# Grouping the rows of an expert sum four at a time instead of two on TensorE

## The chip, the cores and the metric

The kernel runs on one core of one Trainium2 chip. The metric is the device time of one execution in microseconds (us). Its engines run side by side, each through an instruction list of its own in a fixed order, and meet only at semaphores: TensorE (PE, its weight loads PEld), VectorE (DVE), ScalarE (ACT), GpSimd (POOL) and SyncE (SP), which issues DMAs.

## The reference

One decoder layer over 512 prompt tokens and 32 new tokens. Convolution and sparse attention are merged and normed to `h`; behind that stands the channel mixer, whose last lines the change is about. Each token picks 128 of 16384 experts:

```python
def peer_ffn(x2, peer_w_query, peer_keys1, peer_keys2, peer_u, peer_v):
    qh = jnp.einsum('nd,dhk->nhk', x2, peer_w_query)
    ...
    g = jax.nn.softmax(ts, axis=-1)
    u = peer_u[eidx]
    v = peer_v[eidx]
    a = jax.nn.gelu(jnp.einsum('nd,nhed->nhe', x2, u).astype(jnp.float32), approximate=False)
    return jnp.einsum('nhe,nhed->nd', (g * a).astype(v.dtype), v)
```

`u` and `v` are 128 rows of 1024 numbers for each token.

## The kernel before

The tokens are five tiles: four of 128 prompt tokens (0 to 3) and one of 32 new ones (`S_T`). For each tile a front computes projections, convolution and attention, a tail forms `h` (the products with `w_conv_out` and `w_out`, L1404, then the query product with `w_query`, L1524, and the key products, L1539), and a routing on VectorE (from L2009 on) picks the experts of the 8 heads, one head after the other.

**The gathers.** Each tile then needs 128 `peer_u` fetches (one for each expert slot, for all 128 tokens at once) and 128 `peer_v` fetches (one for each token, its 128 expert rows). Each fetch is 128 x 1024 numbers, 0.524 MB, written by one indirect DMA that GpSimd issues at L906 into a place of a ring of 11 (`PLACES`) in SBUF. Below, a row is one such fetch, row i of tile v is ("v", v, i). A `u` row is used up by one VectorE instruction (L2232), a `v` row by TensorE in `expert_pair` (L1820): the token's 128 weights, in one column of a 128 x 32 block that is zero elsewhere, times the 128 x 512 halves of the row, added into PSUM partitions `32*j` to `32*j + 31` with `j = i % 4`. So four rows in sequence go to four different column quarters of the array. Every such product of float32 runs as two passes, so a pair of rows is 8 passes.

**Who may go on.** GpSimd waits before each fetch until the earlier row in the same place has been used (`dotted` or `summed`). TensorE waits for the rows' landing (`row_in`) and, at the first row of four, for `diag_ready`: ScalarE has then copied the weights of that group of four into its block (`column`, L1293), for which it waits in turn until the group two before has been summed.

**The order.** `fetches` writes the queue by hand: the 128 `u` rows of tile 0, then 80 `v` rows of tile 0 alone (`EARLY_V[0]`), then `u` rows of tile 1 mixed with the other `v` rows of tile 0, then 32 `v` rows of tile 1 alone, the mix of tiles 2 and 1, 32 `v` rows of tile 2 alone, the mix of tiles 3 and 2, 32 `v` rows of tile 3, and the rest. While the 80, 32 and 32 rows stand alone, the front and tail of the next tile run: no `u` row can be fetched before the routing of its tile. Every engine merges its strands (fronts, tails, `mixer`) by estimated times at build, so that TensorE's list has a pair of rows between every few matmuls of the tail. GpSimd's list follows the queue.

In the profile's names `rings` is the ring, `acc` the PSUM sum, `z_stages` holds the weight blocks, `late` the expert numbers, `uah` the transposed `h`.

## Time and profile before

| | |
|---|---|
| median of 3 runs | 2096.13 us (2087.34 to 2105.51) |
| the profiled execution | 2089.12 us |
| its span, first to last instruction | 2087.3 us |
| TensorE busy | 1449.6 us |
| VectorE busy | 1282.2 us |
| GpSimd busy | 1205.3 us |
| moved by DMA | 682.74 MB, 327 GB/s over the span |
| granted TensorE clock, mean | 0.84 of 2.4 GHz |

No engine is busy all the time; which one holds up the others changes from stage to stage, so the table has to be read with stretches of the trace. The execution that was profiled lies 7 us under the median.

### The profile page before, as it was taken

To read this page: it belongs to the slowest core of one execution; us is meant where nothing else is said; L and a number is where in the kernel's file an instruction comes from. 1 tells how busy PE (TensorE), PEld (TensorE's weight loads), DVE (VectorE), ACT (ScalarE), POOL (GpSimd) and SP (SyncE) were. 2 spreads that over 40 slices of the span, in tenths; PEclk is the share of its full clock that TensorE was granted. 3 is DMA by queue.
4 is the path that set the end of the run, shared out by engine and by line. 5 is a ranking of instruction groups with operands and counts; after the bars stand their busy time and mean duration, and the time that the engine had idled before them with its cause. 6 is when DMAs were issued, how large, how long until landed. Compare 5 with 4: busy or idle time off the path is not lost.

```text
span 2087.3 us, 19495 instructions
## 1 busy us (share of the span) xinstructions
PE 1449.6 (69%) x6117; PEld 578.3 (28%) x6117; DVE 1282.2 (61%) x3076; ACT 381.6 (18%) x1031; POOL 1205.3 (58%) x1107
## 2 busy tenths in 40 slices
PE   7899999778975657676658777855354356766435
PEld 3554444333320214342112332411111012221101
DVE  4429964881178499848949767577399974112341
ACT  1510011372000352110027221100010002100000
POOL 1003454485566658756766777677576665336664
PEclk9999999988997885688789878997575568889869
DMA  8728999799989978989999899999999979979997
GB/s 305 315 87 304 327 357 367 261 307 324 324 312 341 378 243 296 363 295 329 352 404 336 312 344 372 329 364 373 307 362 349 370 261 392 382 249 358 378 364 293
DMA packets 207458, 682.74 MB, mean 327 GB/s; under 512 B 26901, under 2 KB 54933, under 8 KB 200787
## 3 DMA queue, kind: packets, MB, share of 16 engines
q0 software_dynamic: 157376, 581.67, 76.4%
q1 hardware_dynamic: 42971, 90.66, 12.2%
q10 hardware_dynamic: 7008, 9.17, 1.2%
q8 instruction: 49, 0.80, 0.2%
q14 instruction: 54, 0.44, 0.1%
HBM read 668.88 MB, written 12.94 MB: 327 GB/s over the span
## 4 chain that ended last, share of the span: by engine, by line
PE 33%; DVE 19%; POOL 15%; issue 13%; DMA 8%; SPq 7%; ACT 2%; another core or an unknown queue 2%; POOLq 0%; ACTq 0%; DVEq 0%
POOL rings L906 15%; PE acc L1820 8%; DVE rings L2232 7%; PE acc L1380 7%; DMA rings<-peer_v,late 6%; PE wide L1380 3%; PE bank L1524 3%; DVE small L1884 3%; SPq L707 3%; PE wide L1404 2%; PE acc L1347 2%; SPq L715 2%; DVE uah L1887 1%; DVE soft_score L1887 1%
## 5 line engine op out<-in xcount | busy, mean ns | idle before, releaser
L906 POOL DMA_INDIRECT rings<-peer_u,late x544 | 611.8, 1125 | 428.6 <-DVE late L2232 166.7
L1820 PE MATMUL acc<-rings,z_stages 128*32 128x512 f32 x2048 | 554.5, 704 | 397.6 <-issue 211.4
L906 POOL DMA_INDIRECT rings<-peer_v,late x544 | 585.0, 1075 | 341.2 <-PE acc L1820 154.2
L2232 DVE CUSTOM_DVE_ANT_0 rings<-rings,uah 128x1024 f32<-128x1024 f32 x288 | 346.7, 1224 | 151.6 <-DMA rings<-peer_u,late 136.5
L2232 DVE CUSTOM_DVE_ANT_0 rings<-rings,late 128x1024 f32<-128x1024 f32 x256 | 308.6, 1223 | 99.3 <-DMA rings<-peer_u,late 94.6
L1820 PEld LDWEIGHTS acc<-rings,z_stages 128*32 128x32 f32 x2048 | 120.1, 120 | 771.0 <-issue 763.6
L1380 PE MATMUL acc<-rings 128*128 128x512 f32 (+1 forms) x352 | 147.3, 569 | 0.0
L1293 ACT COPY z_stages<-late 128x4 f32<-128x4 f32 x136 | 26.2, 198 | 523.0 <-PE acc L1820 329.9
L1553 PE MATMUL wide<-zt,ident_s 128*128 128x512 f32 x122 | 73.2, 700 | 20.9 <-issue 11.7
L1380 PEld LDWEIGHTS acc<-rings 128*128 128x128 f32 x352 | 62.5, 190 | 69.6 <-issue 68.9
L1667 PE MATMUL wide<-keep,soft_score 128*128 128x64 f32 x320 | 57.8, 335 | 33.3 <-ACT soft_score L1112 31.2
L1043 ACT ACTIVATE zt<-uah,conv_p 128x128 f32<-128x128 f32 x244 | 76.7, 390 | 18.8 <-PE wide L1553 14.4
L1347 PE MATMUL acc<-rings 128*128 128x512 f32 (+2 forms) x176 | 69.0, 540 | 14.4 <-DMA small<-quarter 12.2
L1380 PE MATMUL wide<-rings,uah 128*128 128x512 f32 (+1 forms) x176 | 74.4, 564 | 0.0
L1667 PEld LDWEIGHTS wide<-keep,soft_score 128*128 128x128 f32 x320 | 51.1, 241 | 70.6 <-ACT soft_score L1112 56.9
L1524 PE MATMUL bank<-uah,w_query_s 128*128 128x128 f32 x512 | 63.6, 281 | 1.5 <-ACT uah L1070 1.4
L1524 PEld LDWEIGHTS bank<-uah,w_query_s 128*128 128x128 f32 x512 | 59.8, 194 | 14.8 <-issue 12.4
L1404 PE MATMUL wide<-w_out_s,uah 128*128 128x512 f32 x128 | 62.5, 637 | 1.4 <-ACT uah L1063 0.7
L1097 ACT ACTIVATE soft_score<-soft_score,small 128x128 f32<-128x128 f32 (+3 forms) x64 | 35.6, 557 | 128.0 <-DVE small L2097 119.0
L1553 PE MATMUL wide<-z_stages,ident_s 128*128 128x512 f32 x64 | 38.3, 683 | 29.6 <-ACT z_stages L1043 28.5
L2009 DVE MAX8 uah<-zt 128x8 f32<-128x128 f32 x68 | 19.3, 284 | 63.7 <-PE bank L1524 49.3
L1636 PE MATMUL bank<-keep,queries 64*128 64x128 f32 (+3 forms) x128 | 54.2, 563 | 0.0
(298 smaller groups left out, 1594.4 us busy)
## 6 DMA issues: line engine op xcount, KB each, us to landing
rings<-w_in SPq DMA_DIRECT2D x36, 1024.0 KB, 7.5
rings<-peer_u,late POOLq DMA_INDIRECT x544
rings<-peer_v,late POOLq DMA_INDIRECT x544
z_rows<-z_stages ACTq DMA_DIRECT2D x30, 256.0 KB
soft_score<-ln SPq DMA_DIRECT2D x6, 1024.0 KB
zt<-z_rows SPq DMA_DIRECT2D x2, 2596.0 KB
w_out_s<-w_out POOLq DMA_DIRECT2D x1, 4096.0 KB, 17.0
w_query_s<-w_query POOLq DMA_DIRECT2D x1, 4096.0 KB, 14.0
```

The source lines that it names most:

```text
L707: return sp.value_load(page_s[0:1, at:at + 1], min_val=0, max_val=N_POOL - 1)
L906: nc.gpsimd.indirect_dma_start(ring[:, place, :], None, table, offs).then_inc(row_in[place], 16)
L1043: last = nc.scalar.activation(scaled_of(t, k)[:, c, :], uT3[:, c, k:k + P], ACT.Copy, scale=cp[:, c, k:k + 1])
L1347: last = nc.tensor.matmul(acc[:, i % 2 * BLK + lo:i % 2 * BLK + hi], xT_0[:, k, :], w[:, c, :], start=(k == 0), stop=(k == KC - 1))
L1380: last = nc.tensor.matmul(z_bank[j][:, 0:width], x[j][:, m, :], w[:, c, :], **flags)
L1404: last = nc.tensor.matmul(dst[0:n, half * BLK:(half + 1) * BLK], lhs[:, c, 0:n], rhs[:, c, half * BLK:(half + 1) * BLK], start=(c == 0), s ...
L1524: last = nc.tensor.matmul(s_bank[hd // 4][:, hd % 4 * P:(hd % 4 + 1) * P], wqu[:, c, hd * PEER_DQ:(hd + 1) * PEER_DQ], aT3[:, c, :], start ...
L1553: nc.tensor.matmul(wide[:, BLK:], ident[:, :], scaled_of(t, k).rearrange("p c n -> p (c n)"), start=(k == 0), stop=(k == CONV_W - 1), skip ...
L1667: last = nc.tensor.matmul(wide[:, o * HEAD_DIM:(o + 1) * HEAD_DIM], pt2[:, g % 2, at * P:(at + 1) * P], v3[:, j, kv * HEAD_DIM:(kv + 1) * ...
L1820: last = nc.tensor.matmul(acc_v[QUAD * j:QUAD * (j + 1), half * BLK:(half + 1) * BLK], lone[:, quad % LONE, j, QUAD - 1 - m:2 * QUAD - 1 - m],
L1884: chain.link(V.max(top, values))
L2232: V.tensor_tensor_reduce(out=ring[:, place, :], in0=ring[:, place, :], in1=h, scale=1.0, scalar=0.0, op0=ALU.mult, op1=ALU.add, accum_out= ...
```

## The change

The 80, 32 and 32 `v` rows of tiles 0, 1 and 2 that stand alone in the queue are multiplied in groups of four: TensorE reaches the group at the place where the second pair stood, waits there for all four rows, and issues the first halves of the four and then the second halves. All other rows, the 32 of tile 3 too, stay in pairs. The semaphore `summed` goes up once for each row as before.

```diff
+    def rows_at_once(v, i):
+
+        return N_QUADS if v < LAST and i < EARLY_V[v] else N_QUADS // 2
+
...
-        def expert_pair(v, i):
+        def expert_rows(v, i, count):
...
-            for k in (i, i + 1):
+            for k in range(i, i + count):
                 place, landed, _ = HOMES["v", v, k]
                 pe.wait_ge(row_in[place], landed)
...
             for half in range(2):
-                for k in (i, i + 1):
+                for k in range(i, i + count):
...
-                    if number % 2:
-                        expert_pair(tile, number - 1)
+                    count = rows_at_once(tile, number)
+                    if number % count == count - 1:
+                        expert_rows(tile, number - count + 1, count)
```

The new lines shift the numbers behind them by 4: L1404 becomes L1408, L1524 L1528, L1820 L1824.

TensorE's list at the start of tile 1's tail, where the transposes of the convolution's norm (L1472, L1479) and the product with `w_conv_out` stand. A row here is a run of matmuls of one line; `x4` at L1820 is a pair of rows (two rows, two halves). Before:

```order
L1667 MATMUL wide<-keep,soft_score 128x64 x4
L1472 MATMUL bank<-ident_s,queries 128x128 x4
L1820 MATMUL acc<-rings,z_stages 32x512 x4
L1479 MATMUL bank<-ident_s,soft_score 128x128 x4
L1820 MATMUL acc<-rings,z_stages 32x512 x4
L1404 MATMUL wide<-w_conv_out_s,conv_acc 128x512 x2
L1820 MATMUL acc<-rings,z_stages 32x512 x4
```

And now:

```order
L1671 MATMUL wide<-keep,soft_score 128x64 x4
L1476 MATMUL bank<-ident_s,queries 128x128 x4
L1483 MATMUL bank<-ident_s,soft_score 128x128 x4
L1824 MATMUL acc<-rings,z_stages 32x512 x8
L1408 MATMUL wide<-w_conv_out_s,conv_acc 128x512 x4
L1824 MATMUL acc<-rings,z_stages 32x512 x8
```

The first pair of each four has moved down to the second: the transposes now stand next to each other, and four matmuls of the product stand between groups where two stood between pairs.

TensorE's list at the end of the same tail, in the query product of tile 1. Before:

```order
L1524 MATMUL bank<-uah,w_query_s 128x128 x12
L1820 MATMUL acc<-rings,z_stages 32x512 x4
L1524 MATMUL bank<-uah,w_query_s 128x128 x8
L1820 MATMUL acc<-rings,z_stages 32x512 x4
L1524 MATMUL bank<-uah,w_query_s 128x128 x4
L1539 MATMUL bank<-peer_keys_s,queries 128x128 x8
L1524 MATMUL bank<-uah,w_query_s 128x128 x8
L1820 MATMUL acc<-rings,z_stages 32x512 x4
L1524 MATMUL bank<-uah,w_query_s 128x128 x8
L1820 MATMUL acc<-rings,z_stages 32x512 x8
L1539 MATMUL bank<-peer_keys_s,queries 128x128 x8
L1820 MATMUL acc<-rings,z_stages 32x512 x112
```

And now:

```order
L1824 MATMUL acc<-rings,z_stages 32x512 x8
L1528 MATMUL bank<-uah,w_query_s 128x128 x12
L1543 MATMUL bank<-peer_keys_s,queries 128x128 x8
L1528 MATMUL bank<-uah,w_query_s 128x128 x8
L1824 MATMUL acc<-rings,z_stages 32x512 x8
L1528 MATMUL bank<-uah,w_query_s 128x128 x8
L1824 MATMUL acc<-rings,z_stages 32x512 x8
L1543 MATMUL bank<-peer_keys_s,queries 128x128 x8
L1824 MATMUL acc<-rings,z_stages 32x512 x112
```

Ahead of the last piece of the query product stand 15 groups of four now, and stood 30 pairs before: the same 60 rows.

TensorE's list in the query product of tile 2, with the rows of tile 1. Before:

```order
L1820 MATMUL acc<-rings,z_stages 32x512 x4
L1524 MATMUL bank<-uah,w_query_s 128x128 x16
L1820 MATMUL acc<-rings,z_stages 32x512 x4
L1524 MATMUL bank<-uah,w_query_s 128x128 x12
L1820 MATMUL acc<-rings,z_stages 32x512 x4
L1524 MATMUL bank<-uah,w_query_s 128x128 x12
L1820 MATMUL acc<-rings,z_stages 32x512 x4
L1524 MATMUL bank<-uah,w_query_s 128x128 x8
L1539 MATMUL bank<-peer_keys_s,queries 128x128 x8
L1524 MATMUL bank<-uah,w_query_s 128x128 x4
L1820 MATMUL acc<-rings,z_stages 32x512 x4
L1524 MATMUL bank<-uah,w_query_s 128x128 x12
```

And now:

```order
L1528 MATMUL bank<-uah,w_query_s 128x128 x16
L1824 MATMUL acc<-rings,z_stages 32x512 x8
L1528 MATMUL bank<-uah,w_query_s 128x128 x24
L1824 MATMUL acc<-rings,z_stages 32x512 x8
L1528 MATMUL bank<-uah,w_query_s 128x128 x8
L1543 MATMUL bank<-peer_keys_s,queries 128x128 x8
L1528 MATMUL bank<-uah,w_query_s 128x128 x16
```

Five pairs stood ahead of the end of the query product; two groups of four do now, and the fifth pair has become part of the group behind it. In tile 3's query product three pairs stood there and one group does.

## Rows read from the trace of the kernel before

**Rows 1.** The page: engines' busy time, and the chain that ended last.

```profile
PE 1449.6 (69%) x6117; PEld 578.3 (28%) x6117; DVE 1282.2 (61%) x3076; ACT 381.6 (18%) x1031; POOL 1205.3 (58%) x1107
...
PE 33%; DVE 19%; POOL 15%; issue 13%; DMA 8%; SPq 7%; ACT 2%; another core or an unknown queue 2%; POOLq 0%; ACTq 0%; DVEq 0%
```

**Rows 2.** The page's groups: busy and mean ns, then idle before and its releaser.

```profile
L1820 PE MATMUL acc<-rings,z_stages 128*32 128x512 f32 x2048 | 554.5, 704 | 397.6 <-issue 211.4
L906 POOL DMA_INDIRECT rings<-peer_v,late x544 | 585.0, 1075 | 341.2 <-PE acc L1820 154.2
```

**Rows 3.** Windows: us, busy of PE, PEld, DVE, ACT, POOL, PEclk, DMA share, GB/s.

```profile
480.00:600.00 120.00, 110.92 (x558) 44.55 (x556) 27.58 (x83) 17.90 (x40) 65.78 (x70) 1.00 0.88 314
...
900.00:960.00 60.00, 46.82 (x275) 26.19 (x277) 26.67 (x82) 10.42 (x23) 30.72 (x30) 0.84 0.80 276
```

**Rows 4.** Timeline of TensorE in tile 1's tail: start, us, instruction, passes, idle before.

```profile
501.63 1.98 PE L1404 MATMUL wide<-w_conv_out_s,conv_acc 128*128 128x512 f32 x4
503.55 1.91 PE L1820 MATMUL acc<-rings,z_stages 128*32 128x512 f32 x8
...
547.99 1.94 PE L1820 MATMUL acc<-rings,z_stages 128*32 128x512 f32 x16
...
580.79 1.91 PE L1820 MATMUL acc<-rings,z_stages 128*32 128x512 f32 x8
582.63 2.05 PE L1524 MATMUL bank<-uah,w_query_s 128*128 128x128 f32 x16
```

**Rows 5.** Windows of line L1820 alone, up to the query product's last piece.

```profile
480.00:582.70 102.70, 52.62 (x240) 10.92 (x240) 1.00 0.89 320
```

**Rows 6.** Timeline of VectorE: the routing of tile 1 begins.

```profile
584.72 0.30 DVE L2009 MAX8 uah<-zt 128x8 f32<-128x128 f32 x1 [31.48 <-PE bank L1524]
```

**Rows 7.** Timeline of GpSimd: rows 10 and 11 of tile 0.

```profile
476.68 0.94 POOL L906 DMA_INDIRECT rings<-peer_v,late  x1 [0.30 <-issue]
482.81 0.93 POOL L906 DMA_INDIRECT rings<-peer_v,late  x1 [5.19 <-PE acc L1820]
```

**Rows 8.** Timeline of GpSimd: row 79 of tile 0, first `u` row of tile 1.

```profile
598.58 0.94 POOL L906 DMA_INDIRECT rings<-peer_v,late  x1 [1.65 <-PE acc L1820]
599.82 0.94 POOL L906 DMA_INDIRECT rings<-peer_u,late  x1 [0.30 <-issue]
```

**Rows 9.** Windows of all engines, columns as in rows 3, where the mix runs.

```profile
600.00:620.00 20.00, 11.20 (x42) 2.50 (x40) 17.80 (x62) 0.59 (x3) 14.14 (x15) 0.91 0.99 368
...
680.00:720.00 40.00, 25.66 (x104) 8.11 (x104) 16.40 (x32) 14.11 (x37) 25.49 (x27) 0.85 1.00 393
```

**Rows 10.** The chain that ended last, in order of time: waits for a landing.

```profile
988.27 6.14 DMA rings<-peer_v,late
...
1056.09 12.75 DMA rings<-peer_v,late
```

**Rows 11.** Timeline of TensorE in tile 2's query product.

```profile
914.96 2.91 PE L1820 MATMUL acc<-rings,z_stages 128*32 128x512 f32 x8
...
921.57 1.91 PE L1820 MATMUL acc<-rings,z_stages 128*32 128x512 f32 x8
...
937.55 1.91 PE L1820 MATMUL acc<-rings,z_stages 128*32 128x512 f32 x8
939.40 2.94 PE L1524 MATMUL bank<-uah,w_query_s 128*128 128x128 f32 x24
```

**Rows 12.** Timeline of GpSimd: the first `u` row of tile 2.

```profile
960.14 0.93 POOL L906 DMA_INDIRECT rings<-peer_u,late  x1 [0.30 <-issue]
```

**Rows 13.** Timeline of TensorE in tile 3's query product.

```profile
1322.65 2.17 PE L1820 MATMUL acc<-rings,z_stages 128*32 128x512 f32 x8
...
1333.08 1.91 PE L1820 MATMUL acc<-rings,z_stages 128*32 128x512 f32 x8
1334.92 2.05 PE L1524 MATMUL bank<-uah,w_query_s 128*128 128x128 f32 x16
```

**Rows 14.** Timeline of GpSimd: the first `u` row of tile 3.

```profile
1361.85 0.94 POOL L906 DMA_INDIRECT rings<-peer_u,late  x1 [0.30 <-issue]
```

## The prediction

> **What bounds the kernel now.** I read the page first. No engine is busy throughout, and the chain that ended last runs over TensorE for 33% of the span, VectorE for 19%, GpSimd for 15% [rows 1]: the bound changes with the stage, so the change is worth what it is worth in the stages it touches. The groups name its line: the products of the `v` rows are the dearest group of TensorE, and GpSimd's `v` fetches stood idle for 154.2 us because `acc` L1820 had not given back a place [rows 2].
>
> Then the stage in which the 80 rows stand alone. From 480 to 600 us TensorE is busy for 110.92 of 120 us, VectorE for 27.58, GpSimd for 65.78, and DMA moves 314 GB/s [rows 3]. The timeline shows a rhythm: a piece of the tail's product, 1.98 us, a pair of rows, 1.91 us, and again with no gap [rows 4]. Meanwhile VectorE waits 31.48 us for the query product before the routing of tile 1 can begin at 584.72 [rows 6], and the rows fill the ring and wait: after row 10 GpSimd stood idle for 5.19 us until a pair gave back its places [rows 7]. So TensorE is the bound from 481 to 585 us, with the tail of tile 1 behind it, on which the routing, and through it all later `u` rows, depend. What shortens TensorE's list here moves everything behind it. From 600 us on the picture is another: the DMA engines are 0.99 to 1.00 busy at 368 to 393 GB/s [rows 9].
>
> **The cost of a group of four.** A pair has 8 passes and takes 1.91 us. In a few places the list has pairs next to each other with their rows landed, and there 16 passes take 1.94 us [rows 4]: the four column quarters already work at once when TensorE has four rows in hand. A group of four is exactly that, so I take 1.94 us for it, against 3.8 us for two pairs that are apart. The products per row, their passes and the 512-column width don't change.
>
> The Trainium skill, TensorE: Matmul & The Clock Gate, under Part 3: Packing small matmuls, reports less than full scaling for such packing: 2.38 times with three column tiles of 32 and 3.07 times with four row tiles. An estimate by that page: a group of four would take some 2.4 us rather than 1.94, and the gain worked out below would be about 7 us smaller. The x16 row here says the packing is nearly free in this kernel, and the sum goes by the row.
>
> **Tile 1's tail, step by step.** Up to the last piece of the query product, which starts at 582.63 [rows 4], 240 passes of L1820, 30 pairs, are busy for 52.62 us [rows 5]; that includes those that already overlap. Fifteen groups at 1.94 us are 29.1 us: **23.5 us less**. Not all of it arrives. In two places (the convolution's norm and the norm of `h`) TensorE waits for VectorE and ScalarE, and pairs had filled that time; the first pair of a four has now moved behind the wait. I charge one group, 2 us: 21.5 us.
>
> Next comes the supply of rows. With TensorE faster, rows 11 to 59, which waited for their places from 482.81 us on [rows 7], must land some 20 us sooner. They are 49 x 0.524 = 25.7 MB, and the tail's own loads (`x_rows`, `ln1`) 1.6 MB. At the 368 GB/s of the near-saturated window [rows 9] that takes 74 us and ends at 557 us, and TensorE now wants row 59 at about 559: just in time. In the middle it is not: TensorE wants row 47 after some four fifths of the gain, at about 538 us, and rows 11 to 47 with the loads, 21 MB, need 57 us from 482.8, so 540. Places that come back four at a time add some. A tail delayed there stays delayed. I charge 3.5 us and take **18 us** for the start of the routing. The bounds: 21.5 if the supply keeps up, and below, if the queue gives only the 314 GB/s of the stage now, nearly nothing, since rows 11 to 59 would land at 570 us and the last piece follow at about 576: 8 us.
>
> GpSimd must arrive as well, since the first `u` row of tile 1 stands behind row 79. It was issued at 599.82, 117 us after row 11 [rows 7, 8]. Rows 11 to 79 and the loads are 37.8 MB, 103 us at 368 GB/s, so row 79 lands at 586, is issued some 6 us before that [rows 10], and the `u` row follows at 581: 19 us sooner. Both paths agree, so 18 us. VectorE has 31.48 us of idle time there [rows 6] and only starts sooner. GpSimd issues no more and no fewer fetches.
>
> **Tile 2.** Here 32 rows stand alone, and DMA has room: 0.80 busy, 276 GB/s [rows 3]. The end of the query product has five pairs ahead of it, the first 2.91 us long, four of 1.91, and two groups of four after the change: 10.6 less 3.9 is 6.7 us [rows 11]. For GpSimd: row 11 goes out when the first group ends, at about 921; from there a group needs the place that the group two before it gives back, plus an issue, a landing of 6.1 us [rows 10] and 1.94 us, so two groups take 8.5 us. That is quicker than GpSimd issues eight rows, 10 us at 0.94 and 0.30 us each [rows 7]. With the row that has to wait for its place each time, 21 issues from 921 on take some 33 us: the first `u` row of tile 2 goes out at 954 in place of 960.14 [rows 12]. I take **6 us**.
>
> **Tile 3.** Three pairs (2.17 and twice 1.91 us) stood ahead of the last piece of the query product, and one group does: 6.0 less 1.94 is 4.1 us [rows 13]. GpSimd gets row 11 out about 2 us later than now, since the first places come back with the second pair's time, and makes it up: by the same steps its `u` row goes out 4 to 5 us before 1361.85 [rows 14]. I take **4 us**.
>
> **What costs nothing.** ScalarE's `column` waits for the group two before; that stands at the same point of TensorE's list as before, because a group ends where its second pair ended. The later use of a group's first two rows delays those places by a pair's slot, which is in the sums above. The rows that aren't grouped keep their instructions. What lies behind the three stretches is bound by queues whose beginnings all move (routing, rows, front of the next tile), so I see no place that holds a clock of its own, and let the gains add up.
>
> **The sum.** 18 + 6 + 4 = 28 us off the profiled execution's 2089.1: 2061. The median lies 7 us higher, so **2068 us**.
>
> **Rivals.**
>
> *The ring is too small for groups of four* (slower). Of 11 places a waiting group holds four, and the last row of a group can be issued only when the group two before has been summed. The rate is then one landing plus an issue and a product for eight rows. At 6.1 us that is harmless, but landings of 12.75 us occur under load [rows 10]: (12.75 + 0.3 + 1.94) / 8 is 1.87 us a row, against 116 us for 68 rows now, 1.70 a row [rows 7, 8]. Pairs in the same ring depend on a landing for ten rows and don't suffer. The point from which it decides is a landing of about 11.4 us. If they all were 12.75: 69 rows x 0.17 + 64 x 0.1 is +18 us, 2114 us. For it speaks that TensorE frees the DMA to run into its own saturation, where landings lengthen; against it, that a landing in the mix, at such rates, still takes 6.14 us [rows 10].
>
> *The DMA takes the gain of the first stage.* The stage's 314 GB/s at a DMA share of 0.88 [rows 3] leaves a factor of 1.14 by share: 357 GB/s rather than 368, and bursts of four lose some. Then stage one gives about 8 us and the others 3 each: 14 us, 2082.
>
> *The gain is given back later.* The mix is bound by DMA and VectorE; if one of them has slack that only the late start of the stage hides, the 28 us shrink to about 15: 2081. I count it with the one before.
>
> *The change doesn't do what it says.* If TensorE overlapped the pairs wherever it matters already, nothing would move: 2096. Against it stands 52.62 us for 30 pairs [rows 5], 1.75 us each, where full overlap would be 0.97.
>
> **How the numbers follow.** Forecast (gain 22 to 34 us): 0.55. DMA or later stages take part (gain 8 to 21 us): 0.27. Nothing moves: 0.11. The ring makes it slower: 0.07. The range is to hold 8 in 10: at the low end the unhindered sum, 21.5 + 6.7 + 5 = 33 us, and a few us because runs of one kernel differ by up to 9 us from their median: 2055. At the high end the case of a partial gain down to 8 us: 2089. A change within 1%, 21 us, can hardly be told from none in this kernel. Faster by over 1%: 0.56; within 1%: 0.40, with the partial gain, no effect and most of the slower case; slower by over 1%: 0.04.
>
> **What would show it.** In the new profile L1824 should show 16 passes in 1.94 us in the first stretch, four matmuls of the product between them; the first MAX8 of tile 1 at about 567 us in place of 584.72, and the first `u` row of tile 1 at about 581; GpSimd's idle time for `acc` well under 154 us; a DMA rate near 360 GB/s from 480 to 580. The `u` rows of tiles 2 and 3 should come 24 and 28 us sooner than now. I am wrong if a group takes clearly over 2 us, if TensorE waits for landings in that stretch for more than about 5 us in all, or if the lead at 600 us has melted by 960.

## The result, and where the time went

The changed kernel takes 2089.18 us (median of 19 runs, 2067.47 to 2097.94), the kernel before, on the same chip, 2098.74 (19 runs, 2087.34 to 2109.32). The ratio is 0.9948, 95% interval 0.9928 to 0.9969: by that ratio it is 10.9 us faster, 6.5 to 15.1 by the interval, where 28 were forecast (the two medians alone are 9.6 us apart). The profiled execution took 2084.76 us (span 2083.0) against 2089.12 for that of before.

The page of the changed kernel, parts 1, 4 and 5 (columns as in [rows 1, 2]; the line numbers have moved by four):

```profile
PE 1420.0 (68%) x6117; PEld 573.4 (28%) x6117; DVE 1281.0 (61%) x3076; ACT 381.4 (18%) x1031; POOL 1219.3 (59%) x1107
...
PE 33%; DVE 21%; POOL 13%; issue 12%; DMA 10%; SPq 7%; ACT 2%; another core or an unknown queue 2%; ACTq 0%; POOLq 0%; DVEq 0%
...
L1824 PE MATMUL acc<-rings,z_stages 128*32 128x512 f32 x2048 | 526.5, 741 | 410.7 <-DMA rings<-peer_v,late 220.2
L910 POOL DMA_INDIRECT rings<-peer_v,late x544 | 586.2, 1077 | 321.2 <-issue 138.7
```

GpSimd's idle time before `v` fetches is no longer put down to `acc` in the first place (119.4 us where it was 154.2, and 27.4 us more that the view can't attribute), and the landings of rows have become what TensorE's products wait for most.

In the stretch of the 80 rows TensorE's timeline reads:

```profile
502.79 1.92 PE L1824 MATMUL acc<-rings,z_stages 128*32 128x512 f32 x16
504.65 3.70 PE L1408 MATMUL wide<-w_conv_out_s,conv_acc 128*128 128x512 f32 x8
508.28 1.92 PE L1824 MATMUL acc<-rings,z_stages 128*32 128x512 f32 x16
...
528.21 1.92 PE L1824 MATMUL acc<-rings,z_stages 128*32 128x512 f32 x16 [1.64 <-DMA rings<-peer_v,late]
530.07 3.70 PE L1408 MATMUL wide<-w_out_s,uah 128*128 128x512 f32 x8
534.26 1.93 PE L1824 MATMUL acc<-rings,z_stages 128*32 128x512 f32 x16 [0.50 <-DMA rings<-peer_v,late]
```

A group of four takes 1.92 us, with two pieces of the tail's product between groups instead of one. New are the waits for landings: 0.50 to 1.64 us, four of them up to 546 us (two are shown), 4.8 us in all. The windows of the same kernel, with the columns of [rows 3]:

```profile
500.00:520.00 20.00, 19.53 (x97) 7.05 (x96) 2.76 (x4) 1.76 (x6) 12.70 (x14) 0.99 0.97 351
...
480.00:600.00 120.00, 95.12 (x570) 43.72 (x572) 33.14 (x100) 17.88 (x41) 72.58 (x76) 0.87 0.94 344
```

From 480 to 600 us TensorE is busy for 95.12 us where it was 110.92 [rows 3], and the DMA engines have gone from 0.88 and 314 GB/s to 0.94 and 344. VectorE's first MAX8 of tile 1, by the timeline:

```profile
575.43 0.29 DVE L2014 MAX8 uah<-zt 128x8 f32<-128x128 f32 x1 [32.14 <-PE bank L1528]
```

It is 9.3 us sooner than in [rows 6]. The first `u` rows of tiles 1, 2 and 3 go out at 591.8, 951.4 and 1353.7 us: 8.1, 8.7 and 8.1 us sooner than in [rows 8, 12, 14]. So the first stretch gives some 8 us and the other two add nothing to it.

Positions in the whole execution carry what happened before them: the issue of row 0 of the 80 came at 463.9 us here and at 460.0 in the kernel before, 3.9 us apart before anything of the change runs. I therefore compare stretches from their own row 0. From the issue of row 0 of `v(0)` to the first MAX8 of tile 1 ("first stretch" from here on) it is 124.7 us before and 111.5 after: 13.2 us, not 9.3. It is this figure against the 18 us forecast, and the two short stretches against their 10, that the experiments take apart.

### The profile page after: what moved, and what is told of

The parts are those of the page before. It is cut to its first block, busy times and chain, and to the rows that moved or that the text cites. A ratio compares the mean times of both kernels' runs of the same rounds, so it can differ in the third digit from the quotient of the medians.

```text
span 2083.0 us, 19494 instructions
## 1 busy us (share of the span) xinstructions
PE 1420.0 (68%) x6117; PEld 573.4 (28%) x6117; DVE 1281.0 (61%) x3076; ACT 381.4 (18%) x1031; POOL 1219.3 (59%) x1107
## 4 chain that ended last, share of the span: by engine, by line
PE 33%; DVE 21%; POOL 13%; issue 12%; DMA 10%; SPq 7%; ACT 2%; another core or an unknown queue 2%; ACTq 0%; POOLq 0%; DVEq 0%
POOL rings L910 13%; DVE rings L2237 8%; PE acc L1824 7%; DMA rings<-peer_v,late 7%; PE acc L1384 7%; PE bank L1528 3%; PE wide L1384 3%; DVE small L1889 3%; SPq L711 3%; PE wide L1408 3%; PE acc L1351 2%; DVE uah L1892 2%; SPq L719 2%; DVE soft_score L1892 1%
## 5 line engine op out<-in xcount | busy, mean ns | idle before, releaser
L910 POOL DMA_INDIRECT rings<-peer_u,late x544 | 624.7, 1148 | 436.0 <-DVE late L2237 168.6
L1824 PE MATMUL acc<-rings,z_stages 128*32 128x512 f32 x2048 | 526.5, 741 | 410.7 <-DMA rings<-peer_v,late 220.2
L1824 PEld LDWEIGHTS acc<-rings,z_stages 128*32 128x32 f32 x2048 | 111.1, 124 | 770.7 <-issue 765.7
L1528 PE MATMUL bank<-uah,w_query_s 128*128 128x128 f32 x512 | 65.3, 290 | 5.7 <-issue 5.0
L1528 PEld LDWEIGHTS bank<-uah,w_query_s 128*128 128x128 f32 x512 | 63.1, 204 | 13.7 <-issue 12.3
L1408 PE MATMUL wide<-w_out_s,uah 128*128 128x512 f32 x128 | 60.7, 627 | 1.5 <-ACT uah L1067 0.7
```

What stands on the lines that cost most here:

```text
L910: nc.gpsimd.indirect_dma_start(ring[:, place, :], None, table, offs).then_inc(row_in[place], 16)
L1408: last = nc.tensor.matmul(dst[0:n, half * BLK:(half + 1) * BLK], lhs[:, c, 0:n], rhs[:, c, half * BLK:(half + 1) * BLK], start=(c == 0), s ...
L1528: last = nc.tensor.matmul(s_bank[hd // 4][:, hd % 4 * P:(hd % 4 + 1) * P], wqu[:, c, hd * PEER_DQ:(hd + 1) * PEER_DQ], aT3[:, c, :], start ...
L1824: last = nc.tensor.matmul(acc_v[QUAD * j:QUAD * (j + 1), half * BLK:(half + 1) * BLK], lone[:, quad % LONE, j, QUAD - 1 - m:2 * QUAD - 1 - m],
```

## The experiments

They ran on four chips, which differ (whether the result's own is one of them isn't recorded): the kernel before took 2091.6 us on the first, 2050.6 on the second, 2047.9 on the third, and 2103.1 and 2099.8 (two sessions) on the fourth. Ratios are to the kernel before on the same chip, in brackets the 95% interval.

### Which of the three stretches gives the gain

`only80` groups in the first stretch alone, `only32s` in the two short ones alone (`only80_b` and `only32s_b` are the same kernels on another chip):

```
-        return N_QUADS if v < LAST and i < EARLY_V[v] else N_QUADS // 2
+        return N_QUADS if v == 0 and i < EARLY_V[v] else N_QUADS // 2        # only80
+        return N_QUADS if 0 < v < LAST and i < EARLY_V[v] else N_QUADS // 2  # only32s
```

> Only the 80 rows of tile 0 go in groups of four; the 32 and 32 rows of tiles 1 and 2 stay in pairs. In the trace of the changed kernel tile 0's stretch brought 8 of the 10 us. If the gains of the three stretches add up and stay, this kernel is 6 to 8 us faster than before (ratio 0.996 to 0.997). If a lead won in one stretch is used up by the next one's waits (the rival: later stages take it back), it is under 3 us.

> Only the 32 rows of tile 1 and the 32 of tile 2 go in groups of four; the 80 of tile 0 stay in pairs. If the stretches add up, this is 3 to 6 us faster than before, and with the other kernel it sums to the 10 us of the full change. If holding four places of eleven costs as much as the shorter TensorE list brings, it is 0 to 2 us.

> Groups of four for the 80 rows of tile 0 alone, again, since chips differ (the kernel before took 2091.6 us on one and 2050.6 on another) and times scatter less on the faster one. If the 80 rows carry all of the gain, the ratio is that of the full change on such a chip, 0.991 on the fast one or 0.992 to 0.995 on the slow one; if the stretches add up it is 3 to 6 us short of it.

> Groups of four for the 32 rows of tiles 1 and 2 alone, again. Additive stretches as I had forecast them: 0.995. Theory now (the fetches, not TensorE's list, set the pace there): 0.998 to 1.000.

Measured: only80 2079.78 us, 0.9922 (0.9891 to 0.9954), and only80_b 2034.67 us, 0.9931 (0.9908 to 0.9955). only32s 2090.32 us, 0.9990 (0.9964 to 1.0016), and only32s_b 2048.29 us, 0.9994 (0.9972 to 1.0016). only80 gained 12 to 16 us where 6 to 8 were expected: within the intervals the whole effect is the first stretch's. The two short ones together give 1.3 us on one chip and nothing on the other, and by the intervals no more than 6 to 8.

`tail_only` takes the groups only as far as tile 1's tail has work for TensorE (64, 12 and 12 rows):

```
-        return N_QUADS if v < LAST and i < EARLY_V[v] else N_QUADS // 2
+        return N_QUADS if v < LAST and i < (64, 12, 12)[v] else N_QUADS // 2
```

> Groups of four only as long as the tail's matmuls stand between the rows: rows 0 to 63 of tile 0 and 0 to 11 of tiles 1 and 2; the rows behind the tail, where TensorE has time and the fetches set the pace, go in pairs. Theory one (the gain was lost in the first stretch to TensorE's half clock and to the supply of rows): the same as the full change within 3 us. Rival (groups hold places where the fetches set the pace): 5 us or more faster than the full change, so 15 us faster than before, with the first u row of tile 2 some 4 us further ahead of where it was.

Measured: 2084.22 us, 0.9934 (0.9900 to 0.9968), no different from only80 within the intervals. Groups behind the tail, where only rows are left on TensorE, add nothing that these runs can tell.

### Does TensorE's clock take it back

In the changed kernel the granted clock fell to half in this stretch (0.75 in the window 480 to 500 and 0.83 in 540 to 560, where the kernel before showed no half clock from 481 to 600): TensorE now has gaps. `gap_pairs` leaves pairs where the gaps are, so that rows fill them; `filler` is the changed kernel with passes over a block of zeros in the gaps, which add zero to `acc`:

```
+        in_gap = v == 0 and (8 <= i < 12 or 40 <= i < 52)
-        return N_QUADS if v < LAST and i < EARLY_V[v] else N_QUADS // 2
+        return N_QUADS if v < LAST and i < EARLY_V[v] and not in_gap else N_QUADS // 2   # gap_pairs
...
+            for _ in range(k):                                                           # filler
+                nc.tensor.matmul(acc[:, 0:BLK], zero, w_out[:, 0:BLK], start=False, stop=False, skip_group_check=True)
```

> As the full change, but rows 8 to 11 and 40 to 51 of tile 0 stay in pairs, so that TensorE has a pair to do while it waits for the convolution's norm and for the norm of h, and its clock need not fall there (in the changed kernel it fell to 0.5 at 490.0, 544.6 and 551.5 us, in the kernel before nowhere from 481 to 600). If the lost part of the first stretch is the half clock, the routing of tile 1 starts 3 to 5 us sooner than in the full change (575.4 us) and the kernel is some 4 us faster than it. If the supply of rows was the limit, TensorE only waits longer for rows afterwards and nothing is won: within 2 us of the full change.

> The full change, with nine matmuls of a zero block (they add 0 to acc) ahead of tile 1's waits for the convolution's norm (five), for h (two) and for h's copies (two), so that TensorE is busy where it idles now. The output is unchanged. Theory one, the half clock costs: the clock stays at 1.0 from 480 to 580, the group behind the norm takes 1.9 us and not 3.64, the product behind it 3.7 and not 4.76, and the routing of tile 1 starts 3 to 5 us sooner, at 571. Rival, the supply of rows is the limit: the clock stays up but TensorE waits as much longer for rows, and the routing starts where it did, within 1.5 us.

> The changed kernel itself once more, on the same chip as the next three. By its own 19 runs it should stand at 0.995 of the kernel before; the first routing of tile 1 in its trace at 572 to 577 us and TensorE's clock at 0.5 for 7 to 17 of the 100 us from 480 on.

Measured: gap_pairs 2084.32 us, 0.9954 (0.9924 to 0.9984). filler 2033.21 us, 0.9921 (0.9896 to 0.9945), beside the changed kernel itself, full_again, at 2033.15 us, 0.9914 (0.9897 to 0.9932). The window of filler:

```profile
480.00:580.00 100.00, 90.55 (x561) 43.02 (x559) 24.82 (x73) 17.68 (x39) 64.50 (x67) 0.98 0.95 368
```

and of full_again:

```profile
480.00:580.00 100.00, 84.58 (x532) 39.00 (x524) 26.28 (x78) 17.67 (x39) 64.88 (x68) 0.92 0.95 362
```

The filler keeps the clock up (0.98 for 0.92), and the first stretch changes from 105.9 to 104.4 us, the time not at all. So on this chip the half clock costs at most some 1.5 us. On a chip where `before` takes 2091.6 us, gap_pairs has 0.96 from 480 to 580 us where the changed kernel's own profile has 0.91, and its first stretch is no shorter (112.4 against 111.5 us). The clock falls where TensorE waits; it isn't why it waits. That theory falls, the 4 us of gap_pairs and the 3 to 5 of filler with it. full_again also gained more (0.9914) than the 0.995 that was expected of it: the chips differ in the gain too, which a later section takes up.

### Does the supply of rows take it back

`half_pairs` and `half_groups` are the kernel before and the changed one with every row of the three stretches fetched in its first half only: 512 of 1024 columns, half the bytes. TensorE multiplies as many columns as before, partly of other values:

```
+            half = f[0] == "v" and f[1] < LAST and f[2] < EARLY_V[f[1]]
+            if half:
+                table = table.rearrange("e (k d) -> (e k) d", k=2)
+            nc.gpsimd.indirect_dma_start(ring[:, place, 0:D_MODEL // (1 + half)], None, table,
+                                         offs).then_inc(row_in[place], 16)
```

> The kernel before, but the 80, 32 and 32 rows that stand alone are fetched as 512 numbers for each token instead of 1024 (from the table seen as 512 wide, so other values), and the second half of the product uses what lies in the ring: half the bytes in the three stretches, the same instructions. TensorE was the bound there, so nothing before 585 us should change: routing of tile 1 at 582 to 585 us, and the kernel within 5 us of before or a few us faster where the rows behind the tail come sooner.

> The changed kernel with the same 144 rows fetched as 512 numbers for each token (half the bytes, other values, the same instructions). If the supply of rows cost the first stretch its gain, TensorE no longer waits for landings, the clock stays up, and the routing of tile 1 starts at 562 to 566 us, some 20 us ahead of the pairs with half rows. If the clock and the waits for VectorE and ScalarE are what costs, it stays at 570 to 575 us.

Measured, on the chip of full_again: half_pairs 2050.34 us, 0.9993 (0.9976 to 1.0010): with pairs the bytes don't matter at all, as the prediction had it. half_groups 2021.96 us, 0.9850 (0.9827 to 0.9873), 28.6 us below this kernel before by the medians, against 17.5 for full_again. Its first routing starts at 565.1 us, where the theory of the supply expected 562 to 566. Its window:

```profile
480.00:580.00 100.00, 86.52 (x558) 40.30 (x556) 27.19 (x81) 18.07 (x41) 66.79 (x69) 0.95 0.66 196
```

The same halving in one place each, by the condition `f[1] == 0` (groups_half80) and `0 < f[1] < LAST` (groups_half32s):

> The full change, with half the bytes for the 80 rows of tile 0 only (rows of 512 numbers, other values). The full change with half the bytes for all 144 rows gained 28.6 us, the full change with whole rows 17.4 on the same chip. If the missing 11 us were lost in the first stretch, this kernel gains 25 us or more; if they were lost in the two short ones, some 18.

> The full change, with half the bytes for the 32 rows of tile 1 and the 32 of tile 2 only. The counterpart: some 18 us if the loss lies in the first stretch, 25 or more if it lies in the short ones, about 22 in each if it is shared.

Measured, on the third chip: groups_half80 2026.66 us, 0.9896 (0.9867 to 0.9924), groups_half32s 2027.83 us, 0.9894 (0.9863 to 0.9926); some 21 and 20 us faster than `before`: neither the 25 for one place nor the 18 for the other, but the case in which the loss is shared. The changed kernel didn't run beside them; only80_b did, with 0.9931, and its interval overlaps with both. So a few us in each place are likely and not shown by the times. Read by stretches it is small: the first stretch takes 104.4 to 105.9 us with whole rows (four traces) and 102.5 and 102.7 with half of them, so the supply holds it up by some 2.4 us.

`extra_pairs` and `extra_groups` turn the test round and add load: behind tile 1's norm loads SyncE issues eight copies of 0.52 MB within the DRAM, for which nothing waits but the end.

```
+            if t == 1:
+                for k in range(8):
+                    sp.dma_start(spare[k], io["peer_u"][P * k:P * (k + 1)]).then_inc(spare_in, 16)
```

> The kernel before, and behind the norm loads of tile 1 SyncE issues eight copies of 0.52 MB within the DRAM, in the stretch of the 80 rows; nothing waits for them but the end. It takes from the DMA engines 4.2 MB read and written, beside 42 MB of rows. Theory of the supply: with pairs TensorE sets the pace and rows land early (the waits for landings in the stretch are small), so the routing of tile 1 starts less than 4 us later than in the kernel before, where it started 124.7 us after v(0,0), and the time stays within 0.3% of before. Theory that the supply doesn't matter to either kernel: the same.

> The changed kernel with the same eight copies in the same place. Theory of the supply: with groups of four the rows set the pace in the stretch, so that all the time that the copies take from the DMA engines shows: 8.4 MB more to move at some 380 GB/s are 20 us of the engines if reads and writes both count and 10 us if only one does, and the routing of tile 1 starts 8 to 16 us later than without them (105 to 112 us after v(0,0)), which takes away most of the gain: ratio 0.995 to 1.001. Theory that TensorE's clock or the issue of the rows on GpSimd set the pace: under 4 us later, and the ratio stays at that of the changed kernel, 0.991 to 0.995.

Measured: extra_pairs 2103.13 us, 1.0012 (0.9990 to 1.0034); extra_groups 2095.62 us, 0.9963 (0.9933 to 0.9993). In the traces the first stretch takes 126.8 us with pairs, 2.1 more than in the kernel before, and 127.7 with groups, 12 more than in the trace of the changed kernel on the same chip (full_third, below) and 12 to 18 more than in all traces of groups on such chips. TensorE in extra_groups:

```profile
508.40 3.64 PE L1830 MATMUL acc<-rings,z_stages 128*32 128x512 f32 x16 [5.30 <-DMA rings<-peer_v,late]
...
517.63 1.92 PE L1830 MATMUL acc<-rings,z_stages 128*32 128x512 f32 x16 [1.46 <-DMA rings<-peer_v,late]
...
522.75 3.20 PE L1830 MATMUL acc<-rings,z_stages 128*32 128x512 f32 x16 [2.17 <-DMA rings<-peer_v,late]
```

Three of its four waits for landings are shown, of 9.3 us in all; with pairs there is one, of 0.7 us. So the pairs have slack in the supply and the groups have next to none: more load lands on their path at once. The traced execution of extra_groups was one of its longer ones, 9.3 us above its median, and the median lost only some 6 us against full_third (0.9935, below) on the same chip, with intervals that overlap; 12 us is therefore an upper figure.

### Why the chips differ

`half_groups_b` is half_groups again, on the fourth chip:

> The changed kernel with every peer_v row of the three lone stretches fetched in its first half only (512 of 1024 columns; TensorE multiplies the same number of columns as before, from other values), as in the run before. Theory of the supply: what is left after the halving doesn't depend on the chip's DMA rate, so the ratio is 0.984 to 0.988 and the first routing starts 101 to 104 us after v(0,0) on any chip, also where the changed kernel gains least. If the chips differ by something else (TensorE's clock, semaphores), this run shows it: 106 us or more.

Measured: 2083.03 us, 0.9912 (0.9878 to 0.9945), and 109.4 us for the first stretch, not 102.7. This is the other answer: with the DMA engines at 0.62 from 480 to 580 us, 7 us are still missing that the supply can't have taken. The timeline shows where they go. First half_groups, at the end of the product with `w_out`: TensorE's last piece and the VectorE step that waits for it.

```profile
531.41 1.98 PE L1412 MATMUL wide<-w_out_s,uah 128*128 128x512 f32 x4
...
533.32 1.92 PE L1828 MATMUL acc<-rings,z_stages 128*32 128x512 f32 x16
...
533.51 0.69 DVE L1957 SCALAR_TENSOR_TENSOR uah<-uah,wide 128x512 f32<-128x512 f32 x1 [9.63 <-PE wide L1412]
...
537.97 1.78 PE L1471 MATMUL bank<-ident_s,uah 128*128 128x128 f32 x8 [2.72 <-DVE uah L1968]
```

and half_groups_b in the same place:

```profile
533.56 1.98 PE L1412 MATMUL wide<-w_out_s,uah 128*128 128x512 f32 x4
...
536.10 1.92 PE L1828 MATMUL acc<-rings,z_stages 128*32 128x512 f32 x16 [0.56 <-issue]
...
540.36 0.69 DVE L1957 SCALAR_TENSOR_TENSOR uah<-uah,wide 128x512 f32<-128x512 f32 x1 [11.61 <-remote]
...
544.82 1.97 PE L1471 MATMUL bank<-ident_s,uah 128*128 128x128 f32 x8 [6.79 <-DVE uah L1968]
```

The piece's record ends at 533.39 and VectorE starts 0.1 us later; on the other chip the record ends at 535.54 and VectorE starts at 540.36, 4.8 us later, the releaser unknown to the view ("remote"). At the end of the first half of the same product ScalarE's `column` and a GpSimd fetch, which wait for groups, and VectorE's step start within 0.11 us of each other, when the pass that VectorE needs has been over for 4.3 us by its record (523.02):

```profile
527.28 0.20 ACT L1301 COPY z_stages<-late 128x4 f32<-128x4 f32 x1 [7.81 <-remote]
527.33 0.69 DVE L1957 SCALAR_TENSOR_TENSOR uah<-uah,wide 128x512 f32<-128x512 f32 x1 [18.76 <-remote]
527.39 0.95 POOL L913 DMA_INDIRECT rings<-peer_v,late  x1 [2.72 <-remote]
```

The ends of matmuls are modelled in these records; here three engines say that TensorE was done later than its records, or that its signals came late. The records can't tell the two apart.

I measured that lag at these two places (start of the VectorE step less the recorded end of the last pass it needs; first and second half of `w_out`) in all traces:

```
pairs, all four chips and the first profile (5 traces)             0.0 and 0.1 in each
groups, chips where before takes some 2050 us (6 traces)           0.0 and 0.1 in each
groups, chips where before takes 2090 to 2103 us:
  changed kernel 2.6, 0.1   only80 0.0, 0.5     tail_only 2.8, 4.0
  gap_pairs      0.0, 1.7   first_pairs 0.0, 2.2   extra_groups 0.2, 1.0
  half_groups_b  4.3, 4.8   zero_groups 0.0, 2.3   full_third 0.0, 2.0
```

At these two places it comes only with groups on these chips. Over whole traces late releases come with these chips, with pairs too, and more of them with groups. "remote" stands where the view finds no recorded end in the 1.5 us before the semaphore changed, and this kernel has no other core to wait for. Nearly all such semaphores here are TensorE's; 1 to 5 in a trace are VectorE's. Counted are waits of over 0.15 us:

```
waits that end with "remote"       whole trace     in the first stretch
chips at ~2050, pairs and groups   0 in all eight  0
other chips, before, extra_pairs   45, 50          1, 2
             only32s               29              1
             groups in the first   51 to 81        1 in extra_groups, 7 to 14 in eight
```

The one in the first stretch of the kernel before is a GpSimd fetch, whose semaphore changed 2.5 us after the recorded end of the pair it waits for:

```profile
564.99 0.94 POOL L906 DMA_INDIRECT rings<-peer_v,late  x1 [2.23 <-remote]
```

So groups aren't needed for the lateness. With pairs it is there and falls seldom into this stretch; with groups it falls there 7 to 14 times, but for extra_groups. The first stretch is longer where it does:

```
first stretch, us                  chips at ~2050              chips at 2090 to 2103
pairs                              122.0, 125.8                124.5, 124.7
groups, whole rows                 104.4, 104.7, 104.9, 105.9  109.4, 111.5, 112.4, 113.4, 114.4, 115.8
groups, half rows                  102.5, 102.7                109.4
```

(gap_pairs and first_pairs, with some pairs left, stand with 112.4 and 113.4; groups_half32s with 104.9.)

Within the right column the length does not follow the lag of the two places: tail_only has a lag of 4.0 us and the shortest stretch, only80 has 0.5 and one of the longest. Of the 7.8 us between the two kinds of chips (112.8 on the mean of six, 105.0 of four) only half, 3.9, has been lost when that VectorE step starts; the other half is lost behind it, in the query product, 35.9 us on the mean up to the MAX8 where the other chips take 32.0. The result's own trace has lost only some 1.3 us at that step (74.3 us after row 0, 73.0 on the mean) and 5.2 behind it, some 3 of these before the query product starts, at the copies of the transposed `h` for which it waits. The transposes (L1467) end by their record at 544.00:

```profile
542.68 1.32 PE L1467 MATMUL bank<-ident_s,uah 128*128 128x128 f32 x8 [1.40 <-DVE uah L1964]
...
546.31 0.58 ACT L1074 COPY uah<-bank 128x512 f32<-128x512 f32 x1 [4.58 <-remote]
549.85 0.58 ACT L1074 COPY uah<-bank 128x512 f32<-128x512 f32 x1 [2.96 <-remote]
```

The second copy starts 5.85 us after that end; in the traces of the other kind of chip it is 0.04 with groups and 0.08 with pairs.

`zero_groups` asks whether it is the load that four quarters at once put on TensorE: in the three stretches both operands of every pass come from a block of zeros (the rows are fetched and waited for, their products left out). `full_third` is the changed kernel beside it.

```
+                                            zero[:, 0:QUAD] if quiet else
                                             lone[:, quad % LONE, j, QUAD - 1 - m:2 * QUAD - 1 - m],
+                                            zero.unsqueeze(1).to_broadcast([P, N_QUADS, P]) if quiet else
                                             ring[:, place, half * BLK:(half + 1) * BLK], start=False,
```

> The changed kernel, in the three lone stretches with both operands of every peer_v pass taken from a block of zeros (same shapes, count, order, waits and releases; the rows are fetched and waited for as before, but their products are left out). Theory of TensorE falling behind its records: in the seven traces of groups of four on chips where this program takes some 2090 us, the VectorE step that waits for the product with w_out starts up to 2.6 to 4.8 us after the recorded end of that product, or the fetches that wait for a group start up to 2.5 us late, and in no trace of pairs, and in none of groups on chips where the program takes some 2050 us, is it over 0.1. If that is the load that four quarters at once put on TensorE, passes over zeros end on time: on such a chip the lateness of L1957 is 0.1 us and the first routing starts 104 to 107 us after v(0,0) instead of 111 to 113. If the lateness comes with the order or count of the passes and not with what they multiply, it stays. On a chip without the lateness both kernels are the same, 104 to 106 us.

> The changed kernel as it is, beside zero_groups on the same chip: 111 to 113 us from v(0,0) to the first routing and a ratio of 0.993 to 0.997 where TensorE falls behind its records, 104 to 106 us and 0.990 to 0.992 where it doesn't.

Measured: zero_groups 2087.02 us, 0.9942 (0.9923 to 0.9961), full_third 2081.72 us, 0.9935 (0.9913 to 0.9958); first stretch 115.8 us in both, lag 2.3 and 2.0. The zeros change nothing: the load of these passes isn't the cause. What makes the releases late on these chips stays open. The records show no cause in the instruction queues' transfers either: the code fetches of this stretch are as many on both kinds of chips and take about 1 us each on either.

### Why the short stretches bring nothing

With groups the first places of the ring come back after row 3 instead of row 1. `first_pairs` leaves the first four rows of each stretch in pairs:

```
-        return N_QUADS if v < LAST and i < EARLY_V[v] else N_QUADS // 2
+        return N_QUADS if v < LAST and N_QUADS <= i < EARLY_V[v] else N_QUADS // 2
```

> The changed kernel, but the first four rows of each of the three lone stretches stay in pairs, all others of them in fours. Theory of the late first release: with groups of four the first places of the ring come back after row 3 and not after row 1, so that GpSimd issues row 11 some 1.5 to 4 us later than before (22.7 us after row 0 before, 26.9 in the changed kernel, in tile 1; 17.0 and 18.4 in tile 2). If that is what keeps the 32-row stretches from giving anything, the u row of tile 2 comes some 2 us sooner after v(1,0) than in the changed kernel (56 to 57 us instead of 58.9), that of tile 3 about 1 us sooner, and the ratio to the kernel before is 0.989 to 0.992 on a chip where the changed kernel has 0.991 to 0.995. Theory of the supply: GpSimd then only waits for the same rows a little later in the stretch, and the time is that of the changed kernel, to 0.2%.

Measured: 2098.83 us, 0.9981 (0.9954 to 1.0009), and 62.0 us from row 0 of `v(1)` to the first `u` row of tile 2, where 56 to 57 were expected. Row 11 did go out sooner, 21.5 us after row 0 where full_third on the same chip has 26.2, and the `u` row didn't follow (61.6 there). The theory of the late first release falls.

The timeline of GpSimd shows where the gain goes, in two traces without late releases. First full_again, with groups, from the last long wait for a place to the first `u` row of tile 2:

```profile
913.99 0.94 POOL L910 DMA_INDIRECT rings<-peer_v,late  x1 [4.58 <-PE acc L1824]
...
930.72 0.94 POOL L910 DMA_INDIRECT rings<-peer_v,late  x1 [1.79 <-PE acc L1824]
931.96 1.24 POOL L910 DMA_INDIRECT rings<-peer_u,late  x1 [0.30 <-issue]
```

and half_pairs, with pairs and half rows:

```profile
936.93 0.94 POOL L909 DMA_INDIRECT rings<-peer_v,late  x1 [2.51 <-PE acc L1824]
...
951.04 0.95 POOL L909 DMA_INDIRECT rings<-peer_u,late  x1 [0.30 <-issue]
```

A fetch costs GpSimd 0.94 and 0.30 us. With groups that long wait ends 41.9 us after row 0, with pairs 48.9. But with groups 13 fetches stand between it and the `u` row and one more wait for a place, 18.0 us; with pairs it is 11 fetches and no wait, 14.1 us. The places come sooner and four at a time, and GpSimd then has more of its own issue left to do. Of 7.0 us, 3.1 arrive. That this holds in the other traces is argued from these two.

Over all traces the first MAX8 of tile 2 comes 42.4 us after row 0 with groups (eleven traces with whole rows there, 38.5 to 45.1) and 48.3 with pairs (five, one of them with half rows, 45.0 to 50.7): 5.9 us sooner, with a spread as large as the effect; 6.7 were forecast for TensorE. The `u` row comes after 59.4 in place of 61.8: 2.4 us. In tile 3 it is 27.7 for 31.6 us (3.9 sooner) at the MAX8, and 50.3 for 51.1 at the `u` row.

## Why the prediction was wrong, point by point

**TensorE is the bound from 481 to 585 us**: right. Half the bytes gave pairs nothing (0.9993), and TensorE's own stretch shrank when its list did.

**A group of four takes 1.94 us**: right, 1.92 to 1.94 us at the full clock wherever a group runs through, in the changed kernel and in its variants. The estimate from the page's figures (the Trainium skill, TensorE: Matmul & The Clock Gate, Part 3: Packing small matmuls) was some 2.4; the trace doesn't bear that out for four column tiles of 32 with 512 columns. At the half clock a group takes up to 3.64.

**21.5 us off tile 1's tail with the supply free**: right as a sum. With half the bytes, on the chips without a lag, the first stretch falls from 123.9 (the two traces of pairs there) to 102.6, 21.3 us; between half_pairs and half_groups, on one chip, it is 23.1.

**3.5 us for the supply of rows**: near enough, against my first reading. It was 2.4 on those chips (105.0 on the mean, 102.6); extra_pairs and extra_groups show that it is the groups which hang on it. So 18 us for this stretch holds there: 123.9 less 105.0 is 18.9.

**18 us for the chip of the result**: wrong, and the first of two failed steps. The sum took durations from TensorE's records and let whoever waits for TensorE start at the recorded end; late releases stood in it at nothing. The trace of before has them too (45 "remote" waits), but only one in this stretch. With groups they fell there 7 to 14 times. The result's own trace has 13.2 us in place of 18, the mean of such chips 11.8 (124.6 less 112.8), and at the first `u` row it is 10.2 (139.4 less 129.1, where the other chips have 137.6 less 120.0, 17.6). With the bytes halved the stretch was still 7 us longer than on the other chips (109.4 to 102.6), so it isn't the supply. That late releases cost this is shown by the waits behind them (6.79 us in half_groups_b for 2.72, the copy 5.85 us late in the result's trace); how much of the 7.8 us is theirs, and what makes them, is not known.

**6 us in tile 2 and 4 us in tile 3**: wrong, the second failed step and of about the same size. TensorE's own terms were near (5.9 us for 6.7, 3.9 for 4.1). The steps for GpSimd were near too: they put the `u` rows 58.6 and some 49.3 us after row 0, and with groups it is 59.4 and 50.3 on the mean. What failed is what they were taken off: one execution whose `u` rows happened to come after 64.8 and 53.8 us, where pairs take 61.8 and 51.1 on the mean. So the `u` rows came 2.4 and 0.8 us sooner, not 6 and 4 (in the two traces above it is GpSimd's own issue and a last wait that take up the rest); and the kernels with groups there alone measured 0.9990 and 0.9994, some 1 us with an uncertainty of 5.

**The gains add up and persist**: not contradicted. The lead is 8.1 us at the first `u` row and 8.1 at tile 3's; it was neither given back nor added to.

The steps close: 28 us, less 8 in the first stretch (18 forecast, 10.2 at its `u` row), less 7 to 10 in the short ones, is 10 to 13; measured were 10.9, with 6.5 to 15.1 as the interval. On the chip without the lag 28 less 7 to 10 is 18 to 21; measured were 17.5 (13.9 to 21.1). half_groups, with 28.6, reached the number of the forecast only by leaving out half the bytes; that is no support for it.

**The rivals.** The ring did not make it slower: the time is below that of before on every chip. "The DMA takes the gain" named a number near the result (14 us) by luck: it gave the first stretch 8 us and the short ones 3 each, and the supply took 2 to 3 us of the first stretch. "The gain is given back later" (15 us) is near for no better reason: the lead stayed as it was. "Doesn't do what it says" is excluded by the rows.

## What to carry to other kernels

When a change shortens the list of an engine that sets the pace, price it twice: once by that engine's durations, and once by the queue that feeds it when its places come back in bursts. The smaller gain counts. A difference against the position of one instruction in one execution should be held against the spread of that position (61.8 us on the mean of five traces, 64.8 in the one I read). And a few us in one stretch are worth finding by the start of the engines that wait, not by the modelled ends of the one waited for; read at more than one or two places, since the loss may lie behind them.

## What the runs showed of the hardware that I had not expected

- On some chips the engines that wait for TensorE start later than its recorded ends say, by 4.8 us at the end of `w_out` in half_groups_b and 5.85 us at the copies of `h` in the changed kernel's trace. None of the eight traces on the two chips where before takes some 2050 us has a wait that ends as "remote"; each of the twelve others has 29 to 81, with pairs as with groups. At the end of `w_out` it didn't depend on the values multiplied (2.3 us with zeros, 2.0 with the rows).
- The same kernel takes 2048 us on one chip and 2103 on another, 2.7%. Between the changed kernel's profile and full_again's, 54 us apart, the distance grows through the whole program: 9.3 us at tile 1's routing, 18.0 at tile 2's, 26.8 at tile 3's, 41.2 at the first `u` row of the last tile.
- Keeping TensorE's granted clock at 0.98 instead of 0.92 with idle work gained nothing in a stretch in which it waits for others.
